# The order of steps at twelve waits in a two-block transformer kernel on one core

## What is computed

```python
# block 1, per layer
x = x + 0.5 * swiglu_ffn(rms_norm(x, ffn1_norm[l]), ffn1_w1[l], ffn1_w2[l])     # D_FF 2816
h = rms_norm(x, mix_norm[l]);  proj = h @ w_in[l]
y_a = gmlp_mixer(...);  y_b = retention_mixer(...)
y_c = nsa_mixer(n_q, n_kv, n_g, cmp_pos[l], cmp_w1[l], cmp_w2[l])               # compressed + attention
g_a, g_b, g_c = split(sigmoid(h @ w_merge_gate[l] + b_merge_gate[l]))
mix = g_a * (y_a @ w_branch_out[l, 0]) + g_b * (y_b @ w_branch_out[l, 1]) + g_c * (y_c @ w_branch_out[l, 2])
x = x + mix @ w_o[l]
x = x + 0.5 * swiglu_ffn(rms_norm(x, ffn2_norm[l]), ffn2_w1[l], ffn2_w2[l])
# after block 1: x = rms_norm(x, final_norm)
# block 2, per layer
u = rms_norm_2(x, norm_mix_g[layer]);  proj = u @ w_in[layer]
y = [fourier_mix(a_in), gqa_branch(...), mlstm_branch(...), diff_branch(...)]
x = x + (sum_n sigmoid(gates)_n * (y_n @ w_branch[layer, n])) @ w_out[layer]
x = x + conv_ffn(rms_norm_2(x, norm_ffn_g[layer]), w_up[layer], conv_w[layer], conv_b[layer], w_down[layer])
# conv_ffn: a, lin = split(v @ w_up);  a = 3-tap convolution over tokens + bias;  (gelu(a) * lin) @ w_down
# after block 2: the output is rms_norm_2(x, final_norm_g)
```

## Time and profile before

| | us |
|---|---|
| median of 3 runs | 2262.76 |
| lowest, highest | 2261.45, 2266.33 |
| the profiled execution, its own time | 2262.87 |
| its span in the trace | 2261.2 |
| PE busy | 2230.8 |
| DVE, ACT, POOL busy | 1530.8, 1206.9, 66.2 |
| mean granted clock of PE, share of full speed | 0.999 |

### The profile page before, as it was taken

How to read it: one execution, slowest core, us unless ns; L and a number is a source line. 1 busy time by engine, 2 the same in 40 slices (tenths; PEclk the granted TensorE clock), 3 DMA queues, 4 the chain that set the end, 5 groups by cost and what they waited for, 6 DMA issues and landing times.

```text
span 2261.2 us, 30454 instructions
## 1 busy us (share of the span) xinstructions
PE 2230.8 (99%) x12350; PEld 1897.9 (84%) x12350; DVE 1530.8 (68%) x2115; ACT 1206.9 (53%) x1808; POOL 66.2 (3%) x118
## 2 busy tenths in 40 slices
PE   8999999999999999999999999999999999999998
PEld 7888977888888889778888888888888988888887
DVE  6567578665665676786566866786777766776766
ACT  6456456554554564555555655455555554455554
POOL 0000000000000000000000100000000100000000
PEclk9999999999999999999999999999999999999999
DMA  8565543455545655434655534445555444445552
GB/s 282 191 230 186 210 175 138 168 187 191 196 176 195 236 183 198 176 134 170 247 186 187 180 137 168 150 167 179 184 190 181 170 151 167 157 160 180 187 196 99
DMA packets 62803, 409.38 MB, mean 181 GB/s; under 512 B 7976, under 2 KB 9512, under 8 KB 15304
## 3 DMA queue, kind: packets, MB, share of 16 engines
q1 hardware_dynamic: 62664, 407.44, 50.5%
HBM read 405.83 MB, written 2.10 MB: 180 GB/s over the span
## 4 chain that ended last, share of the span: by engine, by line
PE 86%; DVE 9%; ACT 2%; issue 1%; DMA 1%; POOL 1%; SPq 0%; DVEq 0%; POOLq 0%; ACTq 0%
PE bank L625 18%; PE bank L578 18%; PE bank L579 17%; PE bank L580 17%; PE bank L632 9%; DVE w_lo L265 3%; PE bank L388 1%; DVE a_nsa_nm L1755 1%; ACT a_nsa_pr L1774 1%; DVE a_nsa_sc L1751 1%; DVE a_nsa_pr L1741 0%; PE bank L2300 0%; DMA w_raw<-in_tiles 0%; ACT w_hi L245 0%; PE bank L2467 0%
## 5 line engine op out<-in xcount | busy, mean ns | idle before, releaser
L265 DVE TENSOR_TENSOR w_lo<-w_raw,w_hi 128x2048 fp32r<-128x2048 f32 x368 | 837.4, 2284 | 57.1 <-ACT w_hi L245 56.7
L245 ACT ACTIVATE w_hi<-w_raw 128x2048 fp32r<-128x2048 f32 x359 | 684.9, 1911 | 107.3 <-DMA w_raw<-in_tiles 107.2
L625 PE MATMUL bank<-hT,w_hi 128*128 128x512 f32 x1920 | 458.6, 390 | 0.6 <-DVE w_lo L265 0.6
L625 PEld LDWEIGHTS bank<-hT,w_hi 128*128 128x128 f32 x1920 | 356.0, 188 | 72.9 <-DVE w_lo L265 1.4
L578 PE MATMUL bank<-w_hi,hT 128*128 128x512 f32 (+2 forms) x832 | 328.2, 394 | 4.2 <-DVE a_mix L1143 2.5
L580 PE MATMUL bank<-w_hi,hT 128*128 128x512 f32 (+2 forms) x832 | 318.7, 383 | 0.0
L579 PE MATMUL bank<-w_lo,hT 128*128 128x512 f32 (+2 forms) x832 | 318.5, 383 | 0.0
L632 PEld LDWEIGHTS bank<-hT,w_lo 128*128 128x128 f32 x1920 | 247.0, 191 | 9.8
L632 PE MATMUL bank<-hT,w_lo 128*128 128x256 f32 x1920 | 250.0, 283 | 0.0
L578 PEld LDWEIGHTS bank<-w_hi,hT 128*128 128x128 f32 x832 | 156.6, 188 | 42.8 <-issue 13.8
L580 PEld LDWEIGHTS bank<-w_hi,hT 128*128 128x128 f32 x832 | 156.5, 188 | 31.4
(11 more groups left out here) (394 smaller groups left out, 2982.9 us busy)
## 6 DMA issues: line engine op xcount, KB each, us to landing
w_raw<-in_tiles SPq DMA_DIRECT2D x368, 1024.0 KB, 4.8
a_cmp_w<-in_cmp_w SPq DMA_DIRECT2D x2, 2048.0 KB, 7.7
shifted<-in_bias SPq DMA_DIRECT2D x12, 256.0 KB, 6.9
w_raw<-in_tiles SPq DMA_DIRECT2D x8, 256.0 KB, 4.9
a_gm_rows<-in_rows SPq DMA_DIRECT2D x2, 768.0 KB, 7.0
x_res<-in_x SPq DMA_DIRECT2D x2, 512.0 KB, 5.5
a_ret_rows<-in_rows SPq DMA_DIRECT2D x2, 512.0 KB, 8.3
b_rows<-in_rows SPq DMA_DIRECT2D x2, 512.0 KB, 6.3
```

The lines of the kernel that those rows point to most:

```text
L245: act.activation(k.hi[slot][:], k.raw[slot][:], ACT.Copy).then_inc(k.hi_done[slot], 1)
L265: dve.tensor_tensor(k.lo[slot][:], k.raw[slot][:], k.hi[slot][:].bitcast(F32), ALU.subtract).then_inc(k.lo_done[slot], 1)
L625: pe.matmul(bank[:], k.hi[slot][:, w], k.hT[:, c].rearrange("p a s -> p (a s)"), start=c == 0, stop=False)
```

## The change

Nothing is computed differently; instructions of DVE, ACT, PE and SP stand in another order, and a few are issued as two halves. In order of the program:

- `Start`: the transfer of the second 128 tokens of x is issued ahead of two pieces of tile 1, and ACT's squares and DVE's `a_xn` for it move ahead of pieces.
- `Compressed`: a mark `cmp_max` splits three units into one and two, and DVE does the first unit's product ahead of the softmax sum.
- `Attention` (NSA): in each pair of heads the last `w_lo` moves from ahead of the scores to between scores and `weigh`.
- `Columns` roles in `activate`: `b_qkv` and `b_g` of t=0 no longer stand behind the next `w_hi`.
- `Gqa.vector`: the Fourier `fold` stands ahead of the gains and of a `w_lo`.
- `Differential`: a mark `df_first`, so that the first product is ahead of the last `combine`.
- `Ffn.up`: both tiles of the last pair are made by halves, not only the second (j=1). This holds for all six.
- `end_by_columns`: at the two block ends the last down products go by groups of 512 columns, adds and gains follow each column half, the next `w_lo` is done in two halves around `a_xn`, and the transposes of t=0 stand ahead of the last two groups of t=1.

```diff
@@ Ffn.up
-        last = i == FFN_PAIRS - 1 and j == 1
+        last = i == FFN_PAIRS - 1
         for halves in ((0,), (1,)) if last else ((0, 1),):
@@ Ffn.end
+        orders = (((A, 0, 0), (A, 0, 1), (A, 1, 0), (B, 0, 0), (A, 1, 1), (B, 1, 0), (B, 0, 1), (B, 1, 1)),
+                  ((A, 0, 0), (A, 1, 0), (B, 0, 0), (A, 0, 1), (A, 1, 1), (B, 1, 0), (B, 0, 1), (B, 1, 1)))
+        k.ring.ready(pe, self.down_at(A))
+        for t in range(NT):
+            for i, j, n in orders[t]:
+                if t == 0 and n == 0:
+                    if i == B and j == 0:
+                        k.ring.ready(pe, self.down_at(B))
+                    pe.wait_ge(self.glo_done[j], self.base + i + 1)
+                if t == 1 and (i, j, n) == (B, 0, 1) and following is not None:
+                    following.tensor(pe, 0)
+                last = self.down(pe, i, t, j, (n,))
@@ BlockJoin.gains, vector
-        self.add(dve, t)
         for n in range(2):
             ns = slice(n * 512, (n + 1) * 512)
+            self.add(dve, t, n)
             dve.wait_ge(*self.made(t, n))
             dve.tensor_tensor(self.xn[:, t, ns], k.x[:, t, ns], self.grow[:, ns], ALU.mult).then_inc(self.gained, 1)
...
         self.gains(dve, 0)
+        k.ring.lo_half(dve, self.end + 1, 0)
         self.norm.vector_xn(dve, 0)
-        k.ring.lo_to(dve, self.end + 2)
+        k.ring.lo_half(dve, self.end + 1, 1)
         self.norm.vector_lo(dve, 0, 0, 6)
...
-        k.ring.lo_to(dve, self.end + 3)
+        k.ring.lo_to(dve, self.end + 5)
@@ Fill.activate
-        if last_half:
+        if last_half and not (role[0] == "wide" and role[-1] == 0 and isinstance(role[2], Columns)):
             k.ring.hi_to(act, n + SLOTS)
@@ Compressed, DVE and PE
         dve.tensor_tensor(sc[:], sc[:], m[:].unsqueeze(2).broadcast_to(wide), ALU.subtract).then_inc(self.sc_ok, 1)
+        f.vector(dve, "cmp_max")
         dve.wait_ge(self.pr_ok, 1)
...
-        f.tensor(pe, 3)
+        f.tensor(pe, 1)
+        f.mark("cmp_max")
+        f.tensor(pe, 2)
@@ Attention, DVE
-                f.vector(dve, f"nsa{u // 2}")
+                f.vector(dve, f"nsa{u // 2}", lo=False)
...
             if u % 2:
+                f.vector(dve, f"nsa{u // 2}")
                 weigh(u // 2)
@@ Gqa.vector
         link(last)
+        self.fourier.fold(dve)
         for t in range(NT):
             for lo, hi, at in ((0, 512, 0), (512, 640, 64)):
...
         f.vector(dve, "gqa_a1")
-        self.fourier.fold(dve)
@@ Differential, DVE
+        f.vector(dve, "df_first")
         combine(DIFF_HEADS - 1)
@@ Start
-        k.ring.loads_to(sp, 2)
-        sp.dma_start(k.x[:, 1], x[:, 1]).then_inc(self.x_in[1], 16)
+        for q in range(1, PIECES):
+            k.ring.piece_load(sp, 0, q)
+        for q in range(PIECES):
+            if q == 2:
+                sp.dma_start(k.x[:, 1], x[:, 1]).then_inc(self.x_in[1], 16)
+            k.ring.piece_load(sp, 1, q)
...
         for q in range(PIECES):
+            if q == 2:
+                self.root.scalar(act, 1)
             ring.piece_hi(act, 1, q)
-        self.root.scalar(act, 1)
```

More of the change, by code:

```diff
@@ L200, in loads_to @@
             slot, at = self.slot[m], self.places[m]
-            if m < SPLIT:
-                for q in range(m == 0, PIECES):
-                    self.piece_load(sp, m, q)
-                self.loaded = m + 1
-                continue
             if self.before[m]:
@@ L258, in hi_half, with lo_half @@
             self.hi = m + 1
+    def lo_half(self, dve, m, half):
+        k, slot, cols = self.k, self.slot[m], slice(half * TILE // 2, (half + 1) * TILE // 2)
+        assert self.lo == m
+        dve.wait_ge(k.hi_done[slot], self.nth[m])
+        ins = dve.tensor_tensor(k.lo[slot][:, cols], k.raw[slot][:, cols], k.hi[slot][:, cols].bitcast(F32), ALU.subtract)
+        if half:
+            ins.then_inc(k.lo_done[slot], 1)
+            self.lo = m + 1
     def lo_to(self, dve, n):
@@ L454, in vector @@
         k, root = self.k, self.root
-        self.add(dve, 0, True)
+        for n in range(2):
+            self.add(dve, 0, n)
         dve.wait_ge(*self.grow_in)
@@ L462, in vector @@
                                      op1=ALU.mult).then_inc(self.dve_ok, 1)
[L463 removed]
         for n in range(2):
             ns = slice(n * 512, (n + 1) * 512)
+            self.add(dve, 1, n)
             dve.wait_ge(*self.made(1, n))
@@ L515, in scalar @@
         for t in range(NT):
-            for a in range(2):
-                for n in range(2):
-                    at = 4 * t + 2 * a + n
+            for n in range(2):
+                for a in range(2):
+                    at = 4 * t + 2 * n + a
                     ns = slice(n * 512, (n + 1) * 512)
@@ L755, in tensor @@
                 last.then_inc(used(i - 1), 1)
+        if following is None or following.by_columns:
+            self.end_by_columns(pe, following)
+            return
         for t in range(NT):
-            if t and following is None:
-                break
             for i in (N - 2, N - 1):
@@ L887, in split_lo, with add, add_part, add_columns @@
                           ).then_inc(self.glo_done[j], 1)
-    def add(self, dve, t, last=False):
-        k = self.k
-        for n in range(2):
-            if n == 0 or t and last:
-                k.ring.wait_used(dve, self.down_at(FFN_PAIRS - 1), 1 + t + n)
-            xs = k.x[:, t, n * 512:(n + 1) * 512]
-            dve.scalar_tensor_tensor(out=xs, in0=self.acc[t][n][:], scalar=self.res, in1=xs, op0=ALU.mult, op1=ALU.add
-                                     ).then_inc(k.res_ok, 1)
+    def add(self, dve, t):
+        self.k.ring.wait_used(dve, self.down_at(FFN_PAIRS - 1), 1 + t)
+        for n in range(2):
+            self.add_part(dve, t, n)
+    def add_part(self, dve, t, n):
+        k = self.k
+        xs = k.x[:, t, n * 512:(n + 1) * 512]
+        dve.scalar_tensor_tensor(out=xs, in0=self.acc[t][n][:], scalar=self.res, in1=xs, op0=ALU.mult, op1=ALU.add
+                                 ).then_inc(k.res_ok, 1)
+    def add_columns(self, dve, t, n):
+        self.k.ring.wait_used(dve, self.down_at(FFN_PAIRS - 1), 1 + 2 * t + n)
+        self.add_part(dve, t, n)
 class Columns:
@@ L1037, in scalar_to, with vector_to @@
         self.at["act"] = max(self.at["act"], upto)
-    def vector_to(self, dve, upto):
+    def vector_to(self, dve, upto, lo=True):
         for u in range(self.at["dve"], upto):
-            self.combine(dve, u)
+            self.combine(dve, u, lo or u < upto - 1)
         self.at["dve"] = max(self.at["dve"], upto)
+        if lo and upto and self.units[upto - 1][2]:
+            self.k.ring.lo_to(dve, self.units[upto - 1][0] + SLOTS - 1)
     def product(self, pe, u):
@@ L1150, in combine @@
                 dve.tensor_tensor(mix, mix, tmp, ALU.add).then_inc(self.mixed, 1)
-        if last_half:
+        if last_half and lo:
             k.ring.lo_to(dve, n + SLOTS - 1)
@@ L2495, in tensor @@
         for h in range(DIFF_HEADS + 2):
-            f.tensor(pe, 3 if h < DIFF_HEADS else 1)
+            if h == DIFF_HEADS - 1:
+                f.tensor(pe, 1)
+                f.mark("df_first")
+            f.tensor(pe, 3 if h < DIFF_HEADS - 1 else 2 if h < DIFF_HEADS else 1)
             f.mark(f"df{h + 1}")
@@ L2566, in vector @@
             ring.piece_lo(dve, 0, q)
-        ring.piece_lo(dve, 1, 0)
+        for q in range(PIECES - 1):
+            ring.piece_lo(dve, 1, q)
+        norm.vector_xn(dve, 1)
+        ring.piece_lo(dve, 1, PIECES - 1)
         dve.wait_ge(self.made, 1)
         dve.tensor_copy(self.line[:], k.bank[4][0:DIFF_HEADS, :]).then_inc(self.copied, 1)
-        for q in range(1, PIECES):
-            ring.piece_lo(dve, 1, q)
-        norm.vector_xn(dve, 1)
         dve.tensor_reduce(k.four[:], k.ident[:].rearrange("p (q n) -> p n q", q=4), AX.X, ALU.add).then_inc(
@@ L2823, in program @@
                 joins.append(Join(k, second[l].end, second[l].add, root, norm))
-        joins.append(BlockJoin(k, second[-1].end, second[-1].add, second[-1].sum.made, grow1, (grow_in, 16),
+        joins.append(BlockJoin(k, second[-1].end, second[-1].add_columns, second[-1].sum.made, grow1, (grow_in, 16),
                                cols2[:, 0, C2_MIX:C2_MIX + KC], (0, 1, 2, 3), xn1, sq1, sem))
@@ L2852, in program @@
             else:
-                joins.append(LastJoin(k, last[l].add, last[l].sum.made, root, grow2, (grow_in, 32),
+                joins.append(LastJoin(k, last[l].add_columns, last[l].sum.made, root, grow2, (grow_in, 32),
                                       r2.at("last_xg", 30720, [P, D]), sem))
```

45 lines of the change are left out of this document (21 added, 24 removed).

## The result

| | before | after |
|---|---|---|
| median, us | 2263.96 (5 runs) | 2251.53 (5 runs, 2250.99 to 2252.70) |
| span of the profiled execution | 2261.2 | 2249.3 |
| PE busy | 2230.8 | 2228.1 |

The ratio is 0.9947, with a 95% interval of 0.9936 to 0.9957: 12 us faster, where 19.4 were forecast, and outside the forecast's range. The two profiled executions, 2262.87 and 2251.06, differ by 11.8. Most terms of the forecast sum were right, and still it was some 7.5 us too good. PE's list of waits in the changed kernel says where to look; it answers to the earlier trace rows.

The account below looks back on a forecast made before the run. PE was taken as the bound, busy 99%, with only 30.4 us idle to win. Terms summed to 17.8, or 19.4 with 1.6 for the slow clock; 2262.87 less 19.4 gave 2243.5 us, range 2240 to 2250.

Parts of the forecast that it names:

- the fold: In GQA, moving it ahead of gains and a `w_lo` wins 2.1 us; later rotary gains do not make PE wait.
- `b_g`: ACT does the first `b_qkv` and `b_g` pair before a `w_hi`, removing PE's two waits: 2.8 us.
- rival (b): Stalls move instead of going, as inputs are not ready or PE waits at its next use; half the gain, chance 0.11.
- rival (a): The slow clock stretch near the end stays or appears elsewhere, so only 17.8 us are won: 2245.1; chance 0.25.
- The block end: At BlockJoin, work by columns and half a `w_lo` ahead of `hT` shorten PE's waits: 2.0 us, bounds 1.2 to 2.5.
- The opening: In `Start`, x's second half transferred and squared earlier shortens PE's wait for `a_xn`: 1.2 us, bounds 0 to 1.5.
- Compressed: The two `a_mix` products of t=0 move ahead of the row sum, removing PE's two waits: 2.8 us.
- NSA: Scores go before the `w_lo`, which fills DVE's idle time before weigh; PE's two last-pair waits go: 2.8 us.
- rival (c): Slower: NSA's postponed `w_lo` delays weigh in each of 16 pairs, PE waiting each time: 2285.3 us; chance 0.03.
- The wait for `w_lo` at 1265: After the block end, the kept `x_res` moves behind three `w_lo`, removing one of three PE waits: 0.4 us.
- `df_first`: In Differential, `b_f_tmp` and its mix go ahead of the last combine, removing two PE waits: 1.1 us.
- The last up pair: In the feed-forward, making j=0 by halves too starts the convolution's chain 1.84 us earlier: 2.9 us, bounds 1.5 to 4.0.

Follow-up runs that it names:

- the third experiment: The changed kernel, with DVE copying `b_four_m` ahead of the `w_lo` that stood in front of it; 2245.02 us, ratio 0.9918.
- The fifth: The changed kernel with `b_four_m` copied ahead of the `w_lo` and the Fourier fold put back behind the gains and `w_lo`; 2252.86 us, ratio 0.9947.

## Why the prediction was wrong, step by step

**The step that failed** is the fold, in its last sentence: the steps behind it "come later by the fold's own time" and "PE does not wait for anything of theirs in the list". The term itself was right (2.3 for 2.1). The fold did not make the chain longer, 14.3 us before and after; PE only came to its end sooner. What I did not follow was the order on DVE one station further: behind the rope stands a `w_lo` and then the copy of `b_four_m`, for which PE does wait some 8 us on. Its slack was some 0.4 us, to be read in two rows of the trace of before that I did not look up. It does not show in a list of waits, since a place that is in time has no row there. And the same for `b_g`: it gave its 2.9 on PE, but the chain's head, `b_gqa_sq`, stands behind `w_hi` that wait for their transfers, and came 7.0 us earlier (1264.86 for 1271.87) where PE's lead was 9.0. What the two terms gave, 5.3 with the refills, was taken back, 5.4 in two layers. That this chain is the cause is shown by the third experiment: one operation taken out of it, and 4.6 of it were back, and the clock with it. The fifth shows the order of the two places: with the fold late again, the shorter chain gains nothing. Half of rival (b), "the stalls move", was right with its mechanism (PE, arriving earlier, waits at the next use); it had a chance of 0.11. Its price was for half of all terms, and what happened was all of two terms.

**The clock** was rival (a). The slow stretch at the end went, 1.6, as in the sum, and one of 1.7 came behind the new stall of 2.5. The Trainium skill's rule (TensorE: Matmul & The Clock Gate, section "HAM oscillation"), that it takes a longer idle gap than any of these, did not hold here: in this case's traces the drops go with stalls of 1.86 to 2.85 us (last section).

**The block end** was given 2.0 and brought 0.9. The adds and gains by columns did shorten the chain, but the half `w_lo` that was put into DVE's idle time ran beside POOL's sums and held them: 0.99 us for an add that takes 0.19 alone. I had written that it lies "in the 1.82 us in which it waited for POOL", and so free; it was the one place where it was not, since DVE was waiting for POOL, and POOL for DVE. The Trainium skill has this (SBUF — State Buffer, section "SBUF: two separate sides"): a GpSimd operation that reads SBUF and a VectorE operation with two SBUF inputs take turns at a shared pair of ports, each for a whole instruction. The traces agree, with 0.99 and 0.19, 2.18 and 0.29.

**The opening**, 1.2, measured 0.4 in the ledger, of which 0.2 is not its own, and 0.7 and 1.9 by undoing it: open, as said.

**Right, each with what it measured in the ledger, and the forecast:** Compressed 3.0 (2.8), NSA 2.9 (2.8), together 6.2 by undoing them (5.6); the moved `w_lo` in NSA cost nothing in the other pairs, so rival (c) has no support at all. The wait for `w_lo` at 1265, 0.5 (0.4). `b_g` 2.9 (2.8). The fold 2.3 (2.1). `df_first` 1.3 (1.1). The last up pair 3.0 (2.9), and 3.6 by undoing it; its price 0.1 (0.3). They are all a little above because the refill is 0.25 and not 0.16. The refill is shown as busy, which the last paragraph of the prediction had left out: PE's busy time fell by 2.7, with ten waits fewer, though one slow stretch of the clock stayed. The `b_four_m` waits, -5.4 with their refills, and the clock behind the first, -1.7, were given nothing.

## What to carry to other kernels

A list of waits names only the first place at which a late chain is felt. Before counting a removed wait as won, follow the engine that released it to the next thing PE takes from it, and write down the slack there: the gain is bounded by this slack and by what the chain to that place gains itself. Idle time of DVE in which it waits for POOL is no free place for an operation with two SBUF inputs.
